# Experts' up projection of a two-block layer: the order of a half piece's five matmuls, a full-width second token tile, and GpSimd's remainder ahead of its fetches

## The reference

```python
def peer_ffn(xn, w_query, sub_keys, expert_down, expert_up):
    ...
    idx = jnp.take_along_axis(cand_i, best_pos, axis=-1)      # 8 heads x 16 experts per token
    gates = jax.nn.softmax(best_s, axis=-1)
    ...
    def block(args):
        xb, ib, gb = args
        u = expert_down[ib]
        act = jax.nn.gelu(jnp.einsum('tkd,td->tk', u, xb).astype(f32))
        vv = expert_up[ib]
        return jnp.einsum('tk,tkd->td', (gb * act).astype(vv.dtype), vv)
```

## Time and profile before

| | |
|---|---|
| median of 3 runs | 3091.02 us (3085.73 to 3091.17) |
| profiled execution, its own time | 3095.82 us |
| its span, first to last instruction | 3093.5 us |
| mean granted TensorE clock | 0.998 |
| experts' up, first to last matmul | 2489.1 to 3087.5 us |

### The profile page before, as it was taken

The page is one execution under the profiler, slowest core; times in us unless marked ns, Lnnn a source line. Parts: engine busy times, 40 slices in busy tenths (PEclk is TensorE's granted clock), DMA queues, the critical chain, the costliest instruction groups (busy, mean ns, idle before and its releaser), DMA issues.

```text
span 3093.5 us, 48732 instructions
## 1 busy us (share of the span) xinstructions
PE 3069.1 (99%) x15766; PEld 2567.8 (83%) x15766; DVE 1654.9 (53%) x2846; ACT 1671.4 (54%) x2515; POOL 2533.4 (82%) x1980
## 2 busy tenths in 40 slices
PE   9999999999999999999999999999999999999999
PEld 8888888888888887888888888888888877777777
DVE  5469244434410033655632357167772259998887
ACT  5754543433344455444544434477774467777776
POOL 7888989999999998797788889988889977765553
PEclk9999999999999999999999999999999999999999
DMA  6554655555565565454455655555555589999996
GB/s 237 174 169 152 195 177 184 185 187 183 183 204 194 193 201 176 146 187 164 145 164 189 203 184 189 193 180 175 181 178 195 195 316 355 350 345 355 350 362 239
DMA packets 188519, 659.88 MB, mean 213 GB/s; under 512 B 22864, under 2 KB 28112, under 8 KB 187888
## 3 DMA queue, kind: packets, MB, share of 16 engines
q1 hardware_dynamic: 159168, 573.64, 54.3%
q0 software_dynamic: 20480, 67.15, 6.1%
q10 hardware_dynamic: 8752, 17.60, 1.7%
HBM read 649.92 MB, written 8.39 MB: 213 GB/s over the span
## 4 chain that ended last, share of the span: by engine, by line
PE 94%; DVE 3%; POOL 1%; issue 1%; ACT 0%; DMA 0%; POOLq 0%; DVEq 0%; SPq 0%; ACTq 0%
PE ps L2401 30%; PE ps L2405 15%; PE ps L2499 8%; PE ps L2492 8%; PE ps L2494 8%; PE ps L3037 4%; PE ps L3041 4%; PE ps L3038 4%; PE ps L3042 4%; PE ps L3039 4%; PE ps L2557 3%; POOL lo L620 1%; PE ps L2552 0%; PE ps L2621 0%; DVE pos L2153 0%
## 5 line engine op out<-in xcount | busy, mean ns | idle before, releaser
L620 POOL TENSOR_TENSOR lo<-raw,hi 128x512 fp32r<-128x512 f32 x1656 | 2158.3, 1317 | 326.7 <-PE ps L2405 113.2
L2401 PE MATMUL ps<-xx,hi 128*128 128x512 f32 x4288 | 1521.9, 398 | 5.1 <-DVE xx L1333 5.1
L686 ACT ACTIVATE hi<-raw 128x1024 fp32r<-128x1024 f32 x827 | 869.1, 1059 | 841.6 <-PE ps L2405 432.7
L2405 PE MATMUL ps<-xx,lo 128*128 128x256 f32 x4288 | 1202.4, 280 | 1.7 <-POOL lo L620 1.7
L2401 PEld LDWEIGHTS ps<-xx,hi 128*128 128x128 f32 x4288 | 805.8, 188 | 191.3 <-DVE xx L1333 6.6
L2405 PEld LDWEIGHTS ps<-xx,lo 128*128 128x128 f32 x4288 | 810.4, 189 | 2.8 <-POOL lo L620 2.6
L2492 PE MATMUL ps<-hi,xx 128*128 128x512 f32 x608 | 241.1, 397 | 1.6 <-ACT hi L686 1.1
L2494 PE MATMUL ps<-hi,xx 128*128 128x512 f32 x608 | 237.0, 390 | 0.0
L650 POOL DMA_INDIRECT row<-in_stream,row_up x128 | 134.1, 1048 | 102.2 <-DVE ps L2321 80.9
L3037 PE MATMUL ps<-hi,hg 128*128 128x512 f32 x508 | 201.9, 397 | 0.6 <-issue 0.4
L3038 PE MATMUL ps<-hi,hg 128*128 128x512 f32 x508 | 199.6, 393 | 0.0
(11 more groups left out here) (393 smaller groups left out, 4394.7 us busy)
## 6 DMA issues: line engine op xcount, KB each, us to landing
raw<-in_stream SPq DMA_DIRECT2D x955, 512.0 KB, 3.3
raw_up<-in_stream SPq DMA_DIRECT2D x128, 512.0 KB
side_acts<-side ACTq DMA_DIRECT2D x32, 128.0 KB, 2.3
wg<-in_w_gates ACTq DMA_DIRECT2D x1, 2048.0 KB, 8.8
bias<-in_rpb ACTq DMA_DIRECT2D x1, 2048.0 KB, 8.0
gbc<-in_gains ACTq DMA_DIRECT2D x2, 1024.0 KB, 6.0
spill<-hx ACTq DMA_DIRECT2D x4, 512.0 KB, 3.8
row<-in_stream,row_up POOLq DMA_INDIRECT x128
```

The lines of the kernel that those rows point to most:

```text
L620: nc.gpsimd.tensor_tensor(lo[:, k % 2, n], raw[:, k, n], hi[:, k, n].bitcast(F32), ALU.subtract)\
L686: nc.scalar.activation(hi[:, k, :], raw[:, k, :], ACT.Copy).then_inc(hi_done, 1)
L2401: M.matmul(ps[:, b_, :], w_h, xx[:, i_].rearrange("p a t -> p (a t)"), start=first, stop=False)
L2405: return M.matmul(t_bank(b_), w_l, xh[:, i_, :], start=False, stop=last)
```

## The change

Three edits. In `up_piece` tile B comes first: `hl_b` meets the rounded part of the weight and, behind the wait for the remainder, `hl_b` meets the remainder; then tile A: `h_a` with the rounded part, `h_a` with the remainder, `l_a` with the rounded part. The matmul of tile B with the weight's remainder takes the full width of 128 stationary columns instead of 64, so the product of both remainders is added too. In the last piece of each 32 rounds (`last`) tile B's pair is exchanged in the same way. On GpSimd the remainder of round 1 is put ahead of the three waits, and in the loop the remainder of round r + 1 follows the fetches of iteration r.

```diff
             up_lo(0)
+            up_lo(1)
             pool.wait_ge(slots_ready, 1)
             for g in range(4):
                 pool.wait_ge(side_stored[g], 16 * 8)
@@
                     fetch_act(q)
                 for n in rows_at(r + 1):
                     fetch_row(n)
-                up_lo(r)
+                if r + 1 < UPS:
+                    up_lo(r + 1)
@@ up_piece
-                l_a, h_a, h_b, hl_b = (hg[:, slot, k, f] for f in (
-                    slice(0, P), slice(P, 2 * P), slice(2 * P, P + NT), slice(2 * P, 3 * P)))
+                l_a, h_a, hl_b = (hg[:, slot, k, n * P:(n + 1) * P] for n in range(3))
@@
                     if last:
                         ready(r + UP0, k, n)
-                        M.matmul(b[0:QT], h_b, w_l, start=False, stop=False)
-                        ins = M.matmul(b, hl_b, w_h, start=False, stop=True)
+                        M.matmul(b, hl_b, w_h, start=False, stop=False)
+                        ins = M.matmul(b, hl_b, w_l, start=False, stop=True)
@@
-                    M.matmul(a, h_a, w_h, start=first, stop=False)
-                    M.matmul(a, l_a, w_h, start=False, stop=False)
                     M.matmul(b, hl_b, w_h, start=first, stop=False)
                     ready(r + UP0, k, n)
-                    M.matmul(b[0:QT], h_b, w_l, start=False, stop=False)
-                    M.matmul(a, h_a, w_l, start=False, stop=False)\
+                    M.matmul(b, hl_b, w_l, start=False, stop=False)
+                    M.matmul(a, h_a, w_h, start=first, stop=False)
+                    M.matmul(a, h_a, w_l, start=False, stop=False)
+                    M.matmul(a, l_a, w_h, start=False, stop=False)\
                         .then_inc((half_used, unit_used)[n], 1)
```

## The result

The changed kernel takes 3072.15 us, the median of five runs (3071.15 to 3074.45). Five runs of the kernel before, made beside them, have the median 3088.31 (3085.73 to 3091.17; the three shown ahead of the prediction had 3091.02). The ratio is 0.9935, 95% interval 0.9916 to 0.9955: 16.2 us or 0.65% faster.

What follows compares the result with a forecast made beforehand. TensorE, busy 99% of the span, was taken as the bound. Up stage 598.4 - 6.8 - 11.2 + 1.6 = 582.0 us, a gain of 16.4, giving 3075 us; own range 3071 to 3079, widened to 3070 to 3085.

Steps and rivals of the forecast that it cites:

- part 1: GpSimd's round 1 remainder ahead of its fetches, in idle time at no cost, removes round 1's stall: gain 6.8 us.
- the part on VectorE: Up stage: VectorE's round takes 7.1 us, 9.6 if it meets GpSimd's pair; it cannot fall back far, small waits go.
- The stall with its clock: Round 1 of the up stage: 4.35 us wait for GpSimd plus 2.41 us slow clock, 6.8 us in all, goes.
- Pace and small waits: Up stage: matmul spacing falls from 230.9 to 226.8 ns and small waits go, together a gain of 11.2 us.
- The new waits: Up stage: 0.3 us at round 3, 0.7 and 0.2 at round 33, 0.4 for uneven spacings; 1.6 us lost.
- two bounds: Up-stage pace stays at 230.9 ns (gain 0) or reaches 226.8 (gain 11.2 us with small waits); the second was taken.
- The wider loads are hidden: Tile B's remainder weight load grows from 135 to 189 ns, covered by the running matmul; uncovered it would cost 27.4 us.
- The pace staying: Rival: up-stage pace is due to memory traffic and stays, only the stall goes; gain 5 to 8, 3084 us; chance 0.13.
- VectorE locked and late: Rival: VectorE stays locked to GpSimd, 0.5 us late in 28 rounds with rows, 14 us back; 3089 us; chance 0.07.
- Two locks in each round: Rival: VectorE meets the lock twice a round, 12.2 us, 87 over 28 rounds; 3162 us; chance 0.05 with uncovered loads.
- exposed loads: Rival: wider weight loads show, 27.4 us lost less 6.8; 3112 us; chance 0.05 shared with VectorE locked twice a round.
- The stall moving to round 3: Rival: the change does nothing, as the stall moves to round 3, where GpSimd has seven issues first; 3090 us; chance 0.05.

Runs made afterwards that it cites:

- The run with the rows from round 4: Changed kernel with ScalarE's fin_done wait moved to round 33's first copy and gathered rows spread over rounds 4 to 30 instead of 3 to 30: 3072.93 us.
- narrow down projection: Kernel before, with one of six down-projection matmuls on 64 stationary columns instead of 128 in 160 of 176 groups: 3092.77 us, ratio 1.0010.
- width alone: Kernel before, with only tile B's weight-remainder matmul widened from 64 to 128 stationary columns: 3082.70 us, ratio 0.9977.
- 96 columns: Changed kernel with 96 instead of 128 stationary columns in tile B's remainder matmul, outside the last piece of each 32 rounds: 3085.14 us, ratio 0.9987.
- the moved wait: Changed kernel with ScalarE's fin_done wait moved from before round 33's first rounded part to before its first copy into PSUM: 3071.82 us, ratio 0.9942.
- GpSimd's half alone: Kernel before, with only GpSimd's remainder put ahead of its fetches, matmuls unchanged: 3082.23 us, ratio 0.9974.
- order alone: Kernel before, with only the matmuls reordered, tile B first, keeping the 64-column remainder matmul and GpSimd's order: 3090.83 us, ratio 1.0005.

## Why the prediction was right in its sum, and the step that failed

**The step that failed.** The time came out within the range, but one of the prediction's own signs of being wrong did appear: TensorE waits for VectorE in rounds 3 to 30. It stands 0.66 us for VectorE at the start of round 4. The step behind it is in part 1: the remainder ahead of the fetches was to cost nothing, because the fetches "are not used for two rounds", and the part on VectorE then looked at steady rounds alone. VectorE multiplies the first eight gathered activations with their gates at the end of its round 2. Its timeline in the kernel before:

```profile
2518.80 0.41 DVE L2255 TENSOR_TENSOR hg<-gm,hg 128x256 fp32r<-128x256 f32 x1
2519.14 0.15 DVE L2328 TENSOR_TENSOR coef<-act_q,gate_q 128x8 f32<-128x8 f32 x1
```

There the eighth fetch was issued by 2508.4, 10.8 us before VectorE wanted it, and VectorE waited for nothing. Counted from the stage's first matmul, VectorE wants it at 30.1 us before and at 22.4 after, mostly since the stall had held it back. The eighth fetch is issued by 19.3 before and by 20.7 after: the fetches begin 0.9 later and take 0.5 longer. The lead of 10.8 us shrank to 1.7. VectorE stood 3.48 us for the landing, and GpSimd's pair then held it for 2.3 more. The run with the rows from round 4 shows the cause: with that want one round later both are gone, and so is the wait of TensorE.

**The sum was right, 582.0 against 581.9, and so were its large terms.** The stall with its clock was put at 6.8, and 4.35 + 2.41 is what vanished: no wait over 1 us is left in rounds 1 to 3. Pace and small waits were one term, 11.2; measured, on an even stream 0.3 shorter, it was 9.3 of pace and 2.3 of small waits, and 0.2 of pace is left. The new waits were put at 1.6 and are 1.65, and that is luck: the 0.3 put at round 3 did not come, and 0.66 at round 4, which no term had, took its place. There is luck in the 6.8 as well. Its 2.41 us of slow clock are those of one execution; the kernel with the narrow down projection has the same up stage and lost 1.0 us to the clock after the same stall.

**Why round 1 is in time.** The timeline of GpSimd, changed kernel:

```profile
2478.80 2.55 POOL L636 TENSOR_TENSOR lo<-raw,hi 128x512 fp32r<-128x512 f32 x2 [0.50 <-ACT hi L1291]
...
2485.67 3.32 POOL L636 TENSOR_TENSOR lo<-raw_up,hi 128x512 fp32r<-128x512 f32 x2 [4.33 <-ACT hi L1291]
2489.15 1.36 POOL L641 DMA_INDIRECT act_q<-side_acts,row_act  x1 [0.16 <-PE ps L3043]
...
2496.45 2.55 POOL L636 TENSOR_TENSOR lo<-raw,hi 128x512 fp32r<-128x512 f32 x2
...
2507.64 2.56 POOL L636 TENSOR_TENSOR lo<-raw_up,hi 128x512 fp32r<-128x512 f32 x2
```

Round 1's remainder is made in what was idle time, and the fetches follow at 2489.15. That is 7.2 us behind the stage's first matmul; before it was 2495.42 less 2489.1, 6.3. The pair took 3.32 us and not 2.55, so its cover was 0.9 us short. That is part of what made the fetches late for VectorE in round 3, as above.

**The pace was the uncertain term, and it was read rightly.** Of its two bounds the one from the down projection held, and for the reason read at L3041. TensorE's timeline of the changed kernel over the same place of a half:

```profile
2899.95 0.39 PE L3040 MATMUL ps<-lo_x,hg 128*128 128x512 f32 x1
2900.17 0.39 PE L3041 MATMUL ps<-hi,hg 128*128 128x512 f32 x1
2900.40 0.39 PE L3042 MATMUL ps<-lo_x,hg 128*128 128x512 f32 x1
```

The starts are 0.22 and 0.23 apart, without the 0.24 of before. Read over the whole stage of before, the prediction's "exactly at the one narrow matmul" is only partly so: the mean spacing behind L3041 is 233 ns, but behind L3037, L3038 and L3042, which are all full, it is 233, 230 and 229 (spacings up to 245 ns); only behind L3039 is it 226. Two thirds of what the pace costs lie behind full-width matmuls. After, all five are 227. The width alone, the narrow matmul in the down projection and the 96 columns show from three sides that the width is the cause (with the PSUM partitions that go with it). Why a shorter load disturbs its neighbours is not shown by any run.

**The wider loads are hidden,** as taken. The group of weight loads at the matmul that was narrow (count, busy us, mean ns, idle before):

```profile
L3040 PEld LDWEIGHTS ps<-lo,hg 128*128 128x128 f32 x256 | 48.1, 188 | 11.4 <-POOL lo L636 1.3 <-issue 0.2
```

It is 188 ns for 135, in a spacing that got shorter. By the Trainium skill ("TensorE: Matmul & The Clock Gate", LDWEIGHTS) the 64 columns more cost 53 ns; the trace has 53. The loss of 27 us that follows if loads show did not come.

**The waits: the size was right, one of two places wrong.** Round 33's was put at 0.7 + 0.2 and is 0.77 with two after-effects of 0.1; its cause was read rightly, as the moved wait showed. Round 3's was put at 0.3 behind GpSimd's remainder. That came in time. The wait came a round later and through another engine: 0.66 behind VectorE's hidden part for round 4. That is the failed step above. The part on VectorE has a second fault: it said that VectorE's hidden remainder would be mostly at 0.68, no longer meeting GpSimd. Grouped by form, changed kernel:

```profile
L2255 DVE TENSOR_TENSOR hg<-gm,hg 128x512 fp32r<-128x512 f32 x62 | 84.1, 1357 | 0.0
L2257 DVE TENSOR_TENSOR hg<-gm,hg 128x256 fp32r<-128x256 f32 x62 | 59.2, 955 | 0.0
```

The first line's mean is 1357 ns, as before (1366), but the second's was 681 before:

```profile
L2255 DVE TENSOR_TENSOR hg<-gm,hg 128x256 fp32r<-128x256 f32 x62 | 42.2, 681 | 0.0
```

So the hidden part meets GpSimd more often than before, not less: its two operations are held up by over 0.1 us in 43 of 62 rounds for 33, and lose 76 us in all for 60. VectorE is busy 95.89 of 100 us in 2900:3000 where it was 81.21, and TensorE waits for none of it. What held is the bound beside that claim, that the hidden part is ready ahead of its round (put at 1.8 us; measured at 0.9 to 1.7 in most rounds with rows, 0.3 at the least) whether it meets the pair or not. The small waits of rounds 15 to 21 did go, but not because the two engines part. They are gone with GpSimd's half alone and with the order alone, so what removes them stays open. The lock itself shows plainly: the eight-element operation of VectorE takes 2.45 us beside GpSimd's pair, and 0.15 where it runs alone (at 2519.14 in the kernel before). The Trainium skill ("SBUF — State Buffer", Who interferes with whom) says that two such operations block each other for a whole instruction. This trace agrees that the one is blocked, but for longer: VectorE's operation is held until both instructions of the pair are done (2507.64 + 2.56 = 2510.20, and it ends at 2510.23).

**The absolute time.** 3075 is the gain of 16.4 taken from a median of three runs, 3091.0. With two more runs that median is 3088.3, and the changed kernel came out at 3072.2, 16.2 below. The gain was right to 0.2 us and the time 2.9 too high, within its own range of 3071 to 3079. A match to 0.2 us is closer than five runs each can tell: the interval of the ratio, 0.9916 to 0.9955, is a gain of 14 to 26 us. The trace's 16.5 us in the stage is the better measure.

**The rivals.** The pace staying (3084) is ruled out by x443 at 370 GB/s and by x437 at 193. VectorE locked and late (3089) would show as waits in rounds 5 to 30; there are none, though in the kernel with the width alone it costs some 3 us. Two locks in each round (3162) would have made the program slower, and exposed loads (3112) fall with the pace. The stall moving to round 3 (3090) falls with GpSimd's half alone.

## What to carry to other kernels

Where TensorE is the bound, count its matmuls per 100 us in every stage and compare stages with the same kind of instruction: a difference of 2% is found by that count and by no list of waits. If a matmul with fewer stationary columns stands in a stream of full ones, fill it up, here with the product of both remainders: it costs nothing in its own spacing and gave back 18 ns in each of 508 halves, 9.1 us. Put the work that the next round needs ahead of fetches that only later rounds need; but removing a stall brings every later want forward by its length, so check the first use of those fetches against the new times. Judge two engines that block each other by the slack behind them, not by how often they meet.

## What the runs showed of the hardware

- A stationary operand of 64 or of 96 columns makes a group of matmuls longer: five in 1147, 1153, 1151 or 1164 ns instead of 1133, six in 1380 instead of 1360. All had the same 512 moving columns, and the clock was 1.00.
- After a stall of 4.2 to 4.4 us at the same place, TensorE ran at 1.2 GHz for 12 spacings (before), 13 (width alone), 5 (order alone) and 5 (narrow down projection): 1.0 to 2.6 us for one event in one place. A clock term of that size is a draw, and the trace of one execution doesn't give its mean.

Identical code has two paces elsewhere. In the feed-forward stage, whose matmuls come in pairs of 512 and 256 columns, one execution has x569 and another x581 in the same 100 us at clock 1.00. The window of the kernel before:

```profile
700.00:800.00 100.00, 100.00 (x569) 86.30 (x568) 40.38 (x53) 39.60 (x45) 91.03 (x71) 1.00 0.55 185
```

and of the changed one:

```profile
700.00:800.00 100.00, 100.00 (x581) 87.75 (x580) 41.40 (x54) 40.78 (x45) 92.78 (x73) 1.00 0.56 189
```

The kernel with 96 columns shows x570 in 2300:2400, where the changed one has x580, so it isn't tied to a stage or a kernel. This is where the 7.1 us ahead of the stage come from: between 395 and 892 us of the kernel before, the changed one gains 8.8 us on the same matmuls, and 1.7 go the other way in the rest. What sets it stays open.
